# A two-batch encoder layer on one core: when the MLP's residual is loaded, and where VectorE adds weight tiles

## The reference, cut to what matters

```
h = rms_norm(x, norm_mlp)                               # x: 1536 x 1024
x = x + jnp.square(jax.nn.relu(h @ w_ff1)) @ w_ff2      # w_ff1: 1024 x 4096, w_ff2: 4096 x 1024
```

## Time and profile before

| what | value |
|---|---|
| time of 3 runs, median (lowest to highest) | 2325.28 us (2324.91 to 2327.33) |
| the profiled execution | 2325.24 us, of which span 2323.5 us |
| PE busy | 2287.0 us, 98% |
| DVE busy | 1809.7 us, 78% |
| POOL busy | 1339.1 us, 58% |
| ACT busy | 1192.4 us, 51% |
| TensorE's granted clock | 1.00 throughout |
| DMA, hardware queue q1 | 268.62 MB, 37.2% of the 16 engines' time |

### The profile page before, as it was taken

How to read it: one execution, slowest core, us unless ns; L and a number is a source line. 1 busy time by engine, 2 the same in 40 slices (tenths; PEclk the granted TensorE clock), 3 DMA queues, 4 the chain that set the end, 5 groups by cost and what they waited for, 6 DMA issues and landing times.

```text
span 2323.5 us, 43966 instructions
## 1 busy us (share of the span) xinstructions
PE 2287.0 (98%) x14871; PEld 2000.0 (86%) x14871; DVE 1809.7 (78%) x2613; ACT 1192.4 (51%) x1980; POOL 1339.1 (58%) x1113
## 2 busy tenths in 40 slices
PE   8999999999989999999999999999999999999999
PEld 6888888888756666688888889999999999999999
DVE  6888578989878777867676698888888967777776
ACT  7556121121367777844444456555557465555563
POOL 0002864646457777744444446777777877667765
PEclk9999999999999999999999999999999999999999
DMA  5333344443333121165566654333333532222222
GB/s 195 114 125 119 116 122 110 116 123 108 109 89 101 47 60 37 39 205 177 185 201 200 212 176 136 97 97 97 97 98 106 191 128 73 73 73 73 73 73 91
DMA packets 173145, 271.01 MB, mean 117 GB/s; under 512 B 36529, under 2 KB 91057, under 8 KB 172849
## 3 DMA queue, kind: packets, MB, share of 16 engines
q1 hardware_dynamic: 172400, 268.62, 37.2%
q10 hardware_dynamic: 576, 0.27, 0.0%
HBM read 201.13 MB, written 57.67 MB: 111 GB/s over the span
## 4 chain that ended last, share of the span: by engine, by line
PE 89%; DVE 3%; SPq 3%; DMA 2%; ACT 2%; issue 1%; POOL 1%; ACTq 0%; DVEq 0%; POOLq 0%
PE banks L65 9%; PE banks L67 9%; PE banks L66 9%; PE banks L3237 6%; PE banks L3239 6%; PE banks L3240 6%; PE banks L3213 6%; PE banks L3215 6%; PE banks L3216 6%; PE p_acc L65 3%; PE p_acc L66 3%; PE p_acc L67 3%; PE banks L2095 3%; PE banks L2096 3%; PE banks L2064 2%; PE banks L2043 1%
## 5 line engine op out<-in xcount | busy, mean ns | idle before, releaser
L2707 POOL TENSOR_TENSOR t_wlo<-f_sums,t_whi 128x512 fp32r<-128x512 f32 x256 | 360.4, 1410 | 156.7 <-ACT t_whi L2738 156.7
L2995 DVE TENSOR_TENSOR f_x<-banks,f_x 128x384 f32<-128x384 f32 x448 | 245.1, 553 | 94.8 <-PE banks L3240 94.4
L1892 POOL TENSOR_TENSOR a_plo<-a_p 128x512 f16<-128x512 f32 x236 | 248.0, 1059 | 101.4 <-ACT a_p L1938 96.9
L2693 POOL TENSOR_TENSOR t_wlo<-t_wraw,t_whi 128x1024 fp32r<-128x1024 f32 x67 | 164.6, 2457 | 218.8 <-ACT t_whi L2723 218.8
L1938 ACT ACTIVATE a_p<-banks,s_scales 128x512 f32<-128x512 f32 x320 | 248.4, 778 | 82.2 <-PE banks L2096 56.9
L2738 ACT ACTIVATE t_whi<-f_sums 128x512 fp32r<-128x512 f32 x256 | 161.7, 632 | 230.9 <-PE banks L3240 147.1
L3213 PE MATMUL banks<-block,t_whi 128*128 128x384 f32 x720 | 241.7, 336 | 2.6 <-ACT stage L2852 1.5
L3216 PE MATMUL banks<-block,t_wlo 128*128 128x384 f32 x720 | 240.6, 334 | 0.0
L3215 PE MATMUL banks<-block,t_whi 128*128 128x384 f32 x704 | 235.3, 334 | 0.0
L1971 DVE TENSOR_REDUCE stage<-banks 128x1 f16<-128x1024 f32 (+1 forms) x184 | 191.0, 1058 | 43.9 <-PE banks L2064 42.9
L3237 PE MATMUL banks<-block,t_whi 128*128 128x384 f32 x608 | 203.4, 334 | 1.8 <-DVE f_x L2995 1.8
(11 more groups left out here) (428 smaller groups left out, 6840.0 us busy)
## 6 DMA issues: line engine op xcount, KB each, us to landing
t_wraw<-w_tail_t SPq DMA_DIRECT2D x136, 512.0 KB, 4.0
a_quotient<-w_tail_t SPq DMA_DIRECT2D x64, 512.0 KB, 3.8
w_raw<-w_in_t SPq DMA_DIRECT2D x31, 512.0 KB, 3.8
proj_scratch<-s_gate SPq DMA_DIRECT2D x48, 256.0 KB, 2.1
t_graw<-proj_scratch SPq DMA_DIRECT2D x24, 512.0 KB, 3.7
block<-roped_scratch SPq DMA_DIRECT2D x146, 64.0 KB, 2.2
p_sw<-p_qn SPq DMA_DIRECT2D x60, 128.0 KB, 2.1
mix_scratch<-a_quotient SPq DMA_DIRECT2D x48, 128.0 KB, 2.4
```

The lines of the kernel that those rows point to most:

```text
L1892: pool.tensor_tensor(p_lo[s][:], p32[s][:], p_hi[s], ALU.subtract).then_inc(plo_pool, 1)
L2707: pool.tensor_tensor(weights_of(t, ring_lo[t % 4]), source(t), f32(weights_of(t, ring_hi[t % 4])), ALU.subtract).then_inc(lo_pool.sem, 1)
```

## The change

For half 0, SP now issues the residual's two DMAs of s = 0 at item 16, before `load_unit(8)`, and the two of s = 1 at item 19, after `load_unit(9)`; the waits go with the first part. For half 1 both stay at 13 items before. And in VectorE's item, the weight sum moves from step 3 to behind step 6, the eviction.

```
-                    if at == (-4, -13)[h]:
-                        if h == 0:
-                            x1_out.wait(sp, 16 * 4 * NBLK)
-                            sp.wait_ge(sq_ready, NBLK * KD)
-                        else:
-                            sp.wait_ge(y_out, 16 * 2 * KD)
-                        for s in range(2):
+                    for s in range(2):
+                        if at == ((-5, -2), (-13, -13))[h][s]:
+                            if s == 0 and h == 0:
+                                x1_out.wait(sp, 16 * 4 * NBLK)
+                                sp.wait_ge(sq_ready, NBLK * KD)
+                            elif s == 0:
+                                sp.wait_ge(y_out, 16 * 2 * KD)
                             for k in (2 * s, 2 * s + KH):
                                 sp.dma_start(x1f[:, k:k + 2], ...).then_inc(x1f_in[s].sem, 16)
...
-                q, d = divmod(t + 6, 7)
-                if d < 4 and 0 < q < feed.n_sets:
-                    weight_sum(q, d)
                 for pg, back in feed.pairs_near(t, 8, 24):
                     finish(pg, back)
                 for m in SQUARES.get(t, ()):
                     add_squares(m)
                 if t < END and feed.items[t].kind == "f2":
                     evict(t, 0)
+                q, d = divmod(t + 6, 7)
+                if d < 4 and 0 < q < feed.n_sets:
+                    weight_sum(q, d)
```

## The result

The changed kernel is slower: a median of 2331.49 us over 11 runs (2329.07 to 2335.12) against 2326.04 us for 11 runs of the kernel before (2324.65 to 2327.33). The ratio is 1.0025, with a 95% interval of 1.0016 to 1.0034. The forecast was 2326.9 with a range up to 2330.0, so the time lies outside it, on the slower side.

A forecast was written before the change was run, and what follows sets the result against it. TensorE, busy 98% of the span, was taken as the bound, with VectorE's order setting its waits. 2325.24 - 1.79 + 2.14 + 1.30 = 2326.89, forecast 2326.9 us; range 2322.5 to 2330.0, own range 2325.0 to 2328.7.

The forecast's parts named there:

- The residual, -1.79: Half 0's residual DMAs in two parts: the late weight unit's two TensorE waits, items 24 and 25, go, -1.79 us.
- Either edit alone would take the two waits away: Residual split or later sum would each remove the waits at items 24 and 25, so 1.79 us counts once.
- 1794 to 1838 ... 0: End of half 0, VectorE nearly full: three eviction waits stay, 0 us; ends -2.36 and as much the other way.
- Steady f2 items gain nothing: f2 items: no gain; a sum meeting POOL may delay an eviction half a microsecond, but TensorE needs it an item later.
- The steady second pairs, 0: 13 second pairs: second join ends 0.95 later, yet item 48 starts on time, 0.11 us left of 1.06; 0 us.
- the walk: Step-by-step timing of VectorE's sums, joins and low words in a second pair, including its waits for POOL at the port.
- Rival B: Steady second pairs: VectorE over 0.23 us later loses the port to POOL, 1.36 us 13 times, 2344.6; chance 0.13.
- Rival A: Between 1794 and 1838, evictions in front let TensorE through and sums meet POOL less: 2321.1 us; chance 0.17.
- Pair 1, +1.30: Before item 13: the fourth sum loses a near tie with POOL, TensorE loses 1.30 us; other end 0.11.
- pairs 15 and 31, +2.14: Third of three pairs, no slack: second join later, TensorE loses 1.07 us twice, +2.14; 0.90 if no sum met POOL.

The follow-up runs named there:

- e1: The residual's split alone, with VectorE's order of the kernel before: 2323.43 us, ratio 0.9988 against the kernel before.
- e2: The late weight sums alone, with SP's residual DMAs as in the kernel before: 2333.71 us, ratio 1.0034 against the kernel before.
- e3: The changed kernel with the sum back in its old place in items 196 to 223 only: 2328.38 us, ratio 1.0009.
- e4: The changed kernel with the old order in every second f2 block, except those of items 196 to 223: 2329.86 us, ratio 1.0019.
- e5: The changed kernel with half 1's low words (L2953) made ahead of `finish`, sums still late: 2329.89 us, ratio 1.0018.
- e8: The residual's split with VectorE's old order, and half 1's low words moved to items without a sum: 2324.32 us, ratio 0.9996.

## Why the prediction was wrong, step by step

**The residual, -1.79: right.** The traces give -1.8 at items 24 to 26, and e1 shows it by itself. The units landed 3.8 and 4.4 us after their issue, where I had 3.6, and VectorE's first sum of set 4 no longer waits (1429.40). "Either edit alone would take the two waits away" was wrong: e2 keeps the unit's wait on VectorE and pays for it in the ten items behind.

**"1794 to 1838 ... 0": the step that failed, by +4.0 us.** I argued that "the work ahead of it on VectorE is the same in both orders". The instructions are; their time is not. That VectorE stands until POOL is through I had priced in the pairs; here it is in the bound alone, not in the 0. Added up over VectorE's rows of items 197 to 214, the sums take 14.97 us instead of 13.48 and L2953 8.42 instead of 7.22: 2.69 us more on an engine with 0.27 us to spare. Most of the rest is VectorE's idle time at 1810 to 1812, 0.96 us against 0.20 before, behind TensorE's stalls. I had put the bound there at +2.36, "if the sums meet POOL more often", and taken the middle of two signs; it measured +4.0, beyond that bound. e3, with the old order in this stretch alone, has -0.3.

**"Steady f2 items gain nothing ... TensorE needs that eviction a whole item later": failed where a block ends and a pair follows, +2.4 us.** It holds inside a block, apart from the full stretch. A pair's first item has less room: it waits for both evictions of the item two before it, so for the second one half an item sooner than an f2 item would. Of the room before (1.34 us at item 35, 0.14 or 0.15 of it from an eviction's end to TensorE's start) nothing is left, and each of the 12 pairs behind a block pays 0.12 and, through the slower matmul, 0.08 more. e4 took exactly these away.

**The steady second pairs, 0: right, and the walk with it.** Item 48 starts without a wait, 0.69 us earlier than before (1481.98 against 1482.67), and POOL's row with it (1480.81 against 1481.49). Less these 0.69, the walk has the fourth sum at 1480.57, and it starts at 1480.56, 0.25 ahead of POOL's 1480.81 (the walk: 0.23). The second join ends at 1481.15 + 0.56 = 1481.71; with 0.14, TensorE could start at 1481.85, so 0.13 of the 1.06 are left, where the walk left 0.11. Rival B, the slower case of my list, didn't happen: its 0.23 held, and the meetings were lost elsewhere. Rival A named one of those places and had its sign wrong.

**Pair 1, +1.30, pairs 15 and 31, +2.14: the walks hold, but two of the three meetings fell the other way.** At pair 1 the sum came at 1406.69, POOL at 1406.73, and VectorE took 0.68. The pair cost 0.2, near the cheap end of 0.11. The walk of pairs 15 and 31 starts from rows of before in which the low word ahead of the combination had itself stood for POOL, whose subtractions began at 1783.74 and 2253.92:

```profile
1783.77 1.68 DVE L3001 TENSOR_TENSOR block<-stage,block 128x384 fp32r<-128x384 f32 x1
...
2253.95 1.69 DVE L3001 TENSOR_TENSOR f_a<-stage,t_y_lo 128x384 fp32r<-128x384 f32 x1
```

At pair 31 of the changed kernel it stood again (2259.27, 1.68 us), and the third sum then waited for POOL as in the walk:

```profile
2260.93 1.29 POOL L2707 TENSOR_TENSOR t_wlo<-a_quotient,t_whi 128x512 fp32r<-128x512 f32 x1 [0.40 <-ACT t_whi L2738]
...
2261.45 1.31 DVE L2972 TENSOR_TENSOR f_sums<-a_quotient,f_sums 128x512 f32<-128x512 f32 x1
```

Item 419 lost 1.06 us, where the walk has 1.07. (The profile puts this wait down to ScalarE's high word; it ended 0.03 us behind the second join, and both hang on the late sums.) At pair 15 the low word went through in 0.54 (1784.09), VectorE was 1.1 us ahead of the walk, and item 195 gained 0.2. That the price came at one of the two is chance, and the forecast did not say that it hung on this.

The views print hundredths of a microsecond; the trace has nanoseconds. In the eight traces of both kernels, e1 to e5 and e8 this low word meets POOL 16 times at these two places. It went through in the 13 meetings in which it starts 17 to 22 ns behind POOL and stood in the 3 in which it starts 24 to 30 ns behind. The fourth sum shows the same. e3, VectorE, POOL and TensorE ahead of item 419:

```profile
2260.61 1.30 POOL L2707 TENSOR_TENSOR t_wlo<-f_sums,t_whi 128x512 fp32r<-128x512 f32 x1 [0.34 <-ACT t_whi L2738]
2260.62 1.83 DVE L2974 TENSOR_TENSOR f_sums<-a_quotient 128x512 f32<-128x512 f32 x1
...
2263.07 0.41 PE L3219 MATMUL banks<-block,t_whi 128*128 128x384 f32 x1 [1.13 <-DVE banks L3115]
```

and e5 at the same place:

```profile
2261.15 1.84 POOL L2707 TENSOR_TENSOR t_wlo<-f_sums,t_whi 128x512 fp32r<-128x512 f32 x1 [0.34 <-ACT t_whi L2738]
2261.16 0.68 DVE L2974 TENSOR_TENSOR f_sums<-a_quotient 128x512 f32<-128x512 f32 x1
...
2262.47 0.41 PE L3213 MATMUL banks<-block,t_whi 128*128 128x384 f32 x1
```

Both sums start 0.01 us behind POOL in these rows; in nanoseconds it is 17 in e3 and 14 in e5. One waits for POOL's end and takes 1.83 us, the other takes 0.68 and POOL waits instead (1.84). In e4 (17 ns) the sum stood too, in e2 (15 ns) it went through. Item 419 loses 1.0 us in e3 and gains 0.2 in e5. The Trainium skill, SBUF — State Buffer, section "SBUF: two separate sides", says of these two engines' shared ports that whichever starts first holds them. The traces agree that one of the two stands until the other is through. They do not show that the one whose record starts first wins: VectorE's started up to 23 ns later and still went through. Over all such meetings of sums and low words in these eight traces, 12 to 23 ns behind gave both outcomes and 24 to 44 ns always a stand; why the turn lies there, no run shows.

The errors of the pair terms cancel by chance against the pairs behind blocks: 2.3 us less than forecast at pairs 1 and 15, 2.4 more there. What is left is the stretch, +4.0, of the 3.9 us by which the MLP's change in the traces (+5.6) exceeds the forecast's sum (+1.65).

One reckoning of the prediction does not come out: its own range of 2325.0 to 2328.7 is said to follow from the two ends of pair 1 and of the steady pairs, and those give 2325.7 to 2327.9. The measured time lies above either.

What stays open: what moves the two starts by a few nanoseconds from one execution to the next, and how often an execution without a profile falls the one way or the other. The 11 runs of the changed kernel spread over 6 us, 11 of the kernel before over 2.7 and its 28 beside e1 to e4 over 4.4.

## What to carry to other kernels

When an engine is full, the same instructions in another order do not take the same time: price each by whom it will meet at a shared port in its new place, in the full stretch above all. Where a walk starts from a row that had itself stood for the other engine, price it both ways. Check the item at each change of kind by itself, since a grace of "one item later" shrinks there. Two edits that serve one wait should be tried apart: here the first had the whole gain by itself, and the second had all the loss.

## What the runs showed that I had not expected

- Cutting POOL's subtractions to half their columns (some 0.8 us each instead of 1.35 in the changed kernel) gained 6.4 us in the MLP of the kernel before and 14.0 in the changed one, by the table's last row, though POOL is busy just over half of the span. It also emptied TensorE's list of waits almost wholly. A share of 55% to 58% said nothing about that.
- A meeting at the shared ports costs VectorE up to 1.15 us (0.68 against 1.83), and which engine stands turned on a few nanoseconds of recorded start, so that one place adds or drops about 1 us between kernels that do not differ there.
